# A ten-stage float32 transformer kernel: retention's value products and MLA's rotary scores moved from plain float32 to split fp32r products

## The reference, cut to what matters

```python
# MLA, 8 heads: 128 "nope" + 64 rotated features; the rotated key is shared by all heads
q = concatenate([q[..., :128], _rope(q[..., 128:], positions, 10000.0)])
k_pe = _rope(ckv[..., None, 256:], positions, 10000.0)
k = concatenate([k[..., :128], broadcast_to(k_pe, (b, s, 8, 64))])
s = einsum('bqhd,bkhd->bhqk', q_blk, k) * scale      # causal, softmax over k

# retention, 4 heads of key width 256 and value width 512
a = einsum('bhid,bhjd->bhij', qi, ki) * d_intra      # decayed scores
inner = einsum('bhij,bhjv->bhiv', a, vi)             # the values product
...
return (silu(g) * group_normed(y)) @ w_out
```

## Time and profile before

| | |
|---|---|
| time, median of 3 runs | 2537.4 us (2537.21 to 2538.32) |
| the profiled execution's span, first to last instruction | 2535.6 us |
| PE busy | 2519.6 us, 99% |
| POOL busy | 1057.3 us, 42% |
| DVE busy | 997.8 us, 39% |
| ACT busy | 854.4 us, 34% |
| HBM traffic | 230.8 MB, 91 GB/s |
| granted TensorE clock, mean | 0.999 |

### The profile page before, as it was taken

One profiled execution on the slowest core, in us unless ns is written; L12 is line 12 of the kernel. 1 busy time (PEld: TensorE's weight loads), 2 busy tenths in 40 slices (PEclk: granted clock), 3 DMA queues, 4 the chain that ended last, 5 costly groups with the idle time before them and its releaser, 6 DMA issues.

```text
span 2535.6 us, 32083 instructions
## 1 busy us (share of the span) xinstructions
PE 2519.6 (99%) x12155; PEld 2085.4 (82%) x12155; DVE 997.8 (39%) x1795; ACT 854.4 (34%) x1225; POOL 1057.3 (42%) x824
## 2 busy tenths in 40 slices
PE   9999999999999999999999999999999999999998
PEld 7778888888888888888888888888877877888887
DVE  5556444457576344345234222223123023322223
ACT  4444222234565222235234222223232222422222
POOL 4224444444333444444333444444443433444443
PEclk9999999999999999999999999999999999999999
DMA  5212233223213322332221322223322322232222
GB/s 173 69 54 85 99 100 99 93 73 117 74 62 98 100 88 94 99 100 84 83 67 51 125 91 99 99 99 108 100 76 75 100 67 83 92 100 99 97 88 81
DMA packets 164732, 230.78 MB, mean 91 GB/s; under 512 B 14102, under 2 KB 130844, under 8 KB 164508
## 3 DMA queue, kind: packets, MB, share of 16 engines
q1 hardware_dynamic: 164636, 229.43, 27.9%
HBM read 227.32 MB, written 2.10 MB: 90 GB/s over the span
## 4 chain that ended last, share of the span: by engine, by line
PE 50%; issue 30%; POOL 18%; DVE 1%; DMA 0%; POOLq 0%; ACT 0%; SPq 0%
POOL w_lo L669 18%; PE bank L695 8%; PE bank L697 8%; PE bank L696 8%; PE bank L706 4%; PE bank L708 4%; PE bank L707 4%; PE bank L1486 2%; PE bank L1485 2%; PE bank L1487 2%; PE bank L1511 1%; PE bank L1498 1%; PE bank L762 1%; PE bank L962 1%; PE bank L960 1%
## 5 line engine op out<-in xcount | busy, mean ns | idle before, releaser
L669 POOL TENSOR_TENSOR w_lo<-w_raw,w_hi 128x512 fp32r<-128x512 f32 (+1 forms) x820 | 1057.1, 1321 | 1456.0 <-ACT w_hi L1638 1456.0
L1638 ACT ACTIVATE w_hi<-w_raw 128x2048 fp32r<-128x2048 f32 (+1 forms) x205 | 392.3, 1914 | 636.9 <-PE bank L708 390.4
L695 PE MATMUL bank<-h_hi,w_hi 128*128 128x512 f32 x1472 | 575.8, 391 | 0.0
L697 PE MATMUL bank<-h_hi,w_lo 128*128 128x512 f32 x1472 | 572.9, 389 | 0.0
L696 PE MATMUL bank<-h_lo,w_hi 128*128 128x512 f32 x1472 | 572.8, 389 | 0.0
L2172 DVE TENSOR_TENSOR x_residual<-x_residual,bank 128x512 f32<-128x512 f32 x455 | 310.5, 686 | 360.8 <-PE bank L708 313.2
L706 PE MATMUL bank<-w_hi,act_hi 128*128 128x512 f32 x952 | 371.3, 390 | 0.0
L708 PE MATMUL bank<-w_hi,act_lo 128*128 128x512 f32 x952 | 370.4, 389 | 0.0
L707 PE MATMUL bank<-w_lo,act_hi 128*128 128x512 f32 x952 | 370.4, 389 | 0.0
L695 PEld LDWEIGHTS bank<-h_hi,w_hi 128*128 128x128 f32 x1472 | 276.4, 188 | 62.1 <-issue 4.9
L697 PEld LDWEIGHTS bank<-h_hi,w_lo 128*128 128x128 f32 x1472 | 276.3, 188 | 57.9
(11 more groups left out here) (266 smaller groups left out, 2965.4 us busy)
## 6 DMA issues: line engine op xcount, KB each, us to landing
w_raw<-in_ffn_w_in SPq DMA_DIRECT2D x44, 1024.0 KB, 5.1
w_raw<-in_ffn_w_up SPq DMA_DIRECT2D x32, 1024.0 KB, 5.3
w_raw<-in_ffn_w_down SPq DMA_DIRECT2D x32, 1024.0 KB, 4.8
w_raw<-in_ret_w_in SPq DMA_DIRECT2D x24, 1024.0 KB, 5.1
w_raw<-in_ffn_w_out SPq DMA_DIRECT2D x22, 1024.0 KB, 4.8
w_raw<-in_diff_w_qkv SPq DMA_DIRECT2D x12, 1024.0 KB, 5.2
w_raw<-in_fox_w_in SPq DMA_DIRECT2D x12, 1024.0 KB, 5.3
w_raw<-in_ret_w_out SPq DMA_DIRECT2D x8, 1024.0 KB, 5.0
```

The costliest lines, as they stand in the source:

```text
L669: nc.gpsimd.tensor_tensor(m.w_lo[:, sl, at], m.w_raw[:, sl, at], m.w_hi[:, sl, at].bitcast(F32), ALU.subtract)\
L695: mm(out, hi, x[0][:, k, :], start=k == 0, stop=False)
L697: last = mm(out, lo, x[0][:, k, :], start=False, stop=k == kc - 1)
L1638: m.nc.scalar.activation(m.w_hi[:, sl, 0:width], m.w_raw[:, sl, 0:width], ACT.Copy).then_inc(m.sem("w_hi_ready"), 1)
```

## The change

In MLA, `q_two[:, j]` (fp32r) replaces the shared `q_pe` as stationary operand: head j's 64 rows hold the high part of its rotated queries, and the other 64 rows hold their low part. `k_pe` is filled in both heads' rows, and split into `k_high` and `k_rest` once. Two fp32r products per tile, over `k_high` and `k_rest`, replace the plain float32 product. VectorE makes `q_two` at the end of `take_rotated`: two copies of 128x512 and four subtractions of 32x512 whose output partitions differ from their input partitions.

In retention, the decayed scores are split (ScalarE high, VectorE low, in pieces of 512, 512 and 256 columns) and the values are split (ScalarE's eviction writes the high part, VectorE subtracts to get the low part from the bank). Three fp32r products replace each plain one. The two big fp32r buffers are shared by both uses, `work` shrinks, several temporaries move to `tokbuf` (also those of diff and retention rotations), and small column tiles are put together. The positions' second load moves behind `ln0_done`.

```diff
@@ constants
+RA_PARTS = ((0, 512), (512, 512), (1024, 256))
+RA_READY = (1, 3, 4)
@@ memory
+    m.r_hi, m.r_lo = sb("split_hi", [P, 2048], F32R), sb("split_lo", [P, 2048], F32R)
-    work = sb("work", [P, 11520])
+    work = sb("work", [P, 8192])
...
-    m.q_pe, m.k_pe = view(3072, 512), (view(3584, 512), view(5376, 512))
+    m.q_pe, m.k_pe = view(3072, 512), view(3584, 512)
+    m.q_two = m.r_hi[:, 0:1024].rearrange("p (a b) -> p a b", a=2)
+    m.k_high, m.k_rest = m.r_hi[:, 1024:1536], m.r_hi[:, 1536:2048]
...
+    m.rv_hi, m.rv_lo = (r[:, :].rearrange("p (t d) -> p t d", t=TT) for r in (m.r_hi, m.r_lo))
+    m.ra_hi, m.ra_lo = (a[:, 4:7, :].rearrange("p a b -> p (a b)") for a in (m.act_hi, m.act_lo))
@@ SyncE, beside_ffn0
         sp.wait_ge(*m.upto("mla_rope_made", 2))
+        sp.wait_ge(*m.upto("ln0_done", TT))
         sp.dma_start(m.pos.bitcast(I32), d["positions"].broadcast_to([P, T])).then_inc(s("pos_in"), 16)
-        sp.wait_ge(*m.upto("ln0_done", TT))
         layernorm_rows("ffn", 0)
@@ pe_scores
-        pe.wait_ge(*m.upto("mla_pe_in", p + 1))
+        pe.wait_ge(*m.upto("mla_pe_low", 4 * p + 2 * j + 2))
         if head == 0:
-            pe.wait_ge(*m.upto("k_pe_in", 4))
+            pe.wait_ge(*m.upto("k_pe_rest", 1))
...
-            last = mm(out, m.q_pe[:, tile], m.k_pe[j][:, 0:w], start=False, stop=True)
+            mm(out, m.q_two[:, j, tile], m.k_high[:, 0:w], start=False, stop=False)
+            last = mm(out, m.q_two[:, j, tile], m.k_rest[:, 0:w], start=False, stop=True)
@@ pe_retention, tokens (x == "g") and values
-                    left("v_in", TT, t + 1)
+                    left("v_lo", TT, t + 1)
...
-            left_before("decayed", TT, TT)
-            left_before("v_in", TT, TT)
+            left_before("ra_lo", 3, 3)
+            left_before("v_lo", TT, TT)
...
-                    last = mm(b[2 + q][:, :], m.ra[:, at:at + P], m.rv[:, kb, :], start=kb == 0, stop=kb == q)
+                    hi, lo = m.ra_hi[:, at:at + P], m.ra_lo[:, at:at + P]
+                    mm(b[2 + q][:, :], hi, m.rv_hi[:, kb, :], start=kb == 0, stop=False)
+                    mm(b[2 + q][:, :], hi, m.rv_lo[:, kb, :], start=False, stop=False)
+                    last = mm(b[2 + q][:, :], lo, m.rv_hi[:, kb, :], start=False, stop=kb == q)
@@ act_retention
+        def decays_high():
+            for n, (at, w) in enumerate(RA_PARTS):
+                left_before("decayed", TT, RA_READY[n])
+                run(m.ra_hi[:, at:at + w], m.ra[:, at:at + w], ACT.Copy).then_inc(s("ret_ra_hi"), 1)
+
         if project:
             if hs[0]:
                 split([f"ret.k{n}" for n in hs])
+            if attend:
+                decays_high()
             split([f"ret.v0{n}" for n in hs])
+        else:
+            decays_high()
...
-                    run((m.rv if x == "v" else m.rg)[:, t, :], ...
+                    run((m.rv_hi if x == "v" else m.rg)[:, t, :], ...
@@ dve_start
-    for j in range(2):
-        v.memset(m.k_pe[j], 0.0).then_inc(s("pe_clear"), 1)
...
-            v.tensor_tensor(m.k_pe[j][dst, :], turned[src, :], crossed[src, :], ALU.add).then_inc(s("k_pe_in"), 1)
+            v.tensor_tensor(m.k_pe[dst, :], turned[src, :], crossed[src, :], ALU.add).then_inc(s("k_pe_in"), 1)
+    dve.wait_ge(*m.upto("k_pe_in", 4))
+    v.tensor_copy(m.k_high, m.k_pe).then_inc(s("k_pe_high"), 1)
+    dve.wait_ge(*m.upto("k_pe_high", 1))
+    v.tensor_tensor(m.k_rest, m.k_pe, m.k_high.bitcast(F32), ALU.subtract).then_inc(s("k_pe_rest"), 1)
@@ dve_pairs, end of take_rotated
         v.tensor_tensor(m.q_pe, turned, crossed, ALU.add).then_inc(s("mla_pe_in"), 1)
+        dve.wait_ge(*m.upto("mla_pe_in", p + 1))
+        for j in range(2):
+            v.tensor_copy(m.q_two[:, j, :], m.q_pe).then_inc(s("mla_pe_high"), 1)
+        for j in range(2):
+            dve.wait_ge(*m.upto("mla_pe_high", 2 * p + 2))
+            for half in range(2):
+                src = slice(64 * half + 32 * j, 64 * half + 32 * j + 32)
+                dst = slice(64 * half + 32 - 32 * j, 64 * half + 64 - 32 * j)
+                v.tensor_tensor(m.q_two[dst, j, :], m.q_pe[src, :], m.q_two[src, j, :].bitcast(F32), ALU.subtract).then_inc(s("mla_pe_low"), 1)
@@ dve_retention, after the decays, and after take("k") and the lows
+            for n, (at, w) in enumerate(RA_PARTS):
+                left_before("ra_hi", 3, n + 1)
+                v.tensor_tensor(m.ra_lo[:, at:at + w], m.ra[:, at:at + w], m.ra_hi[:, at:at + w].bitcast(F32), ALU.subtract)\
+                    .then_inc(s("ret_ra_lo"), 1)
...
+            for tile in range(TT):
+                dve.wait_ge(*m.upto("ret_v_in", along(i, [TT * h + tile + 1 for h in hs])))
+                v.tensor_tensor(m.rv_lo[:, tile, :], b[(0, 1, 6, 7)[tile]][:, :], m.rv_hi[:, tile, :].bitcast(F32), ALU.subtract)\
+                    .then_inc(s("ret_v_lo"), 1)
```

More of the change, by code:

```diff
@@ L403, in memory @@
     m.q, m.k, m.v = view(0, 1024, 2), view(1024, 1024, 2), view(2048, 1024, TT)
-    m.q_pe, m.k_pe = view(3072, 512), (view(3584, 512), view(5376, 512))
+    m.q_pe, m.k_pe = view(3072, 512), view(3584, 512)
+    m.q_two = m.r_hi[:, 0:1024].rearrange("p (a b) -> p a b", a=2)
+    m.k_high, m.k_rest = m.r_hi[:, 1024:1536], m.r_hi[:, 1536:2048]
     m.probs, m.probs2, m.turned = view(4096, 1280), view(5376, 1280), view(6656, 1280)
-    m.tmp = view(7936, 1536, 3)
+    m.tmp = view(3072, 1024, 2)
+    m.rot_tmp = [tok[:, 512 * n:512 * n + 512] for n in range(2)]
+    m.k_pe_tmp = [m.turned[:, 512 * n:512 * n + 512] for n in range(2)]
+    m.diff_tmp = [tok[:, 512 * n:512 * n + 512] for n in range(4)]
     m.sel = view(5376, 1024, 8)
     m.sel_r, m.c_rows = m.act_hi[:, 2:4, :].rearrange("p a (b n) -> p (a b) n", n=P), m.act_hi[:, 4, :]
-    m.rv, m.rg, m.ra, m.ry, m.rtmp = view(2048, 2048, TT), view(4096, 2048, TT), view(6144, 1280), view(7424, 2048, TT), view(9472, 2048, 4)
+    m.ry, m.rg, m.ra = view(2048, 2048, TT), view(4096, 2048, TT), view(6144, 1280)
+    m.rv_hi, m.rv_lo = (r[:, :].rearrange("p (t d) -> p t d", t=TT) for r in (m.r_hi, m.r_lo))
+    m.ra_hi, m.ra_lo = (a[:, 4:7, :].rearrange("p a b -> p (a b)") for a in (m.act_hi, m.act_lo))
     m.relu, m.square = view(0, 1024, 2), view(1024, 1024, 2)
@@ L412, in memory @@
     m.squares, m.centered = view(4096, D), view(4096 + D, 2 * D, 2)
-    m.rb_q = view(9472, 512)
-    m.pos, m.ang, m.turns = view(9984, 512), view(10496, 512), view(11008, 512)
+    m.rb_q = tok[:, 1536:2048]
+    m.pos, m.ang, m.turns = view(6656, 512), view(7168, 512), view(7680, 512)
     m.rb = sb("rstd_rows", [P, T])
     m.rope_cos, m.rope_sin = sb("rope_cos", [P, T]), sb("rope_sin", [P, T])
+    m.ret_tmp = [tok[:, 2 * D:2 * D + T], tok[:, 2 * D + T:3 * D], m.rope_cos[:, :], m.rope_sin[:, :]]
     m.consts = sb("consts", [P, 6 * P + 4])
@@ L425, in memory @@
     m.neg_max, m.row_sum, m.row_rec = sb("neg_max", [P, 8]), sb("row_sum", [P, 8]), sb("row_rec", [P, 8])
-    m.o_sq, m.o_eps, m.o_std, m.o_rstd = sb("o_sq", [P, TT]), sb("o_eps", [P, 2, TT]), sb("o_std", [P, TT]), sb("o_rstd", [P, TT])
+    o = sb("o_columns", [P, 5 * TT])
+    m.o_sq, m.o_std, m.o_rstd = (o[:, TT * n:TT * n + TT] for n in range(3))
+    m.o_eps = o[:, 3 * TT:5 * TT].rearrange("p (n t) -> p n t", n=2)
     m.lam_in, m.lam = sb("lam_in", [P, 4, 64]), sb("lam", [P, 8])
@@ L429, in memory @@
     m.wf, m.wf_hi, m.wf_lo = sb("wf", [P, KC, 8]), sb("wf_hi", [P, KC, 8], F32R), sb("wf_lo", [P, KC, 8], F32R)
-    m.x_sum, m.x_sq = sb("x_sum", [P, 2 * TT]), sb("x_sq", [P, TT])
-    m.x_neg_mean, m.x_std, m.x_rstd = sb("x_neg_mean", [P, TT]), sb("x_std", [P, TT]), sb("x_rstd", [P, TT])
+    xc = sb("x_columns", [P, 6 * TT])
+    m.x_sum, m.x_sq = xc[:, 0:2 * TT], xc[:, 2 * TT:3 * TT]
+    m.x_neg_mean, m.x_std, m.x_rstd = (xc[:, TT * n:TT * n + TT] for n in (3, 4, 5))
     m.b_f, m.gate_f, m.c_cols = sb("b_f", [P, 8]), sb("gate_f", [P, 6, TT, 8]), sb("c_cols", [P, TT, 8])
-    m.y_stats, m.y_mean = sb("y_stats", [P, TT, 6]), sb("y_mean", [P, TT, 2])
-    m.y_std, m.y_rstd, m.y_shift = sb("y_std", [P, TT]), sb("y_rstd", [P, TT]), sb("y_shift", [P, TT])
+    y = sb("y_columns", [P, 11 * TT])
+    m.y_stats, m.y_mean = (y[:, at:at + TT * n].rearrange("p (t n) -> p t n", t=TT) for at, n in ((0, 6), (6 * TT, 2)))
+    m.y_std, m.y_rstd, m.y_shift = (y[:, TT * n:TT * n + TT] for n in (8, 9, 10))
     return m
@@ L2018, in step @@
                     act.wait_ge(*m.upto("blocks_done", block_done(i, names, t)))
-                    run((m.rv if x == "v" else m.rg)[:, t, :], b[(0, 1, 6, 7)[t]][:, :], ACT.Copy if x == "v" else ACT.Silu)\
+                    run((m.rv_hi if x == "v" else m.rg)[:, t, :], b[(0, 1, 6, 7)[t]][:, :], ACT.Copy if x == "v" else ACT.Silu)\
                         .then_inc(s(f"ret_{x}_in"), 1)
@@ L2133, in dve_start @@
     dve.wait_ge(*m.upto("mla_rope_made", 2))
-    turned, crossed = (m.tmp[:, n, :] for n in range(2))
+    turned, crossed = m.k_pe_tmp
```

(7 more changed lines are left out.)

## The result

The kernel with the change takes **2542.6 us** (median of 20 runs, 2539.1 to 2545.0) against 2538.0 for the kernel before (20 runs beside them, 2537.0 to 2540.3): ratio **1.0016** with a 95% interval of 1.0010 to 1.0021. It is 4.6 us slower (2.5 to 5.3 by the interval). The forecast was 2534.6, range 2530 to 2539. The profiled execution of after has a span of 2540.8 against 2535.6, so the two traces show the whole difference: +5.2.

The account below looks back on a forecast made before the run. PE, busy 99% of the span, was taken as the bound. Products saved 7.2 us in MLA and 6.7 in retention, waits on VectorE added 11.1: -2.8 from 2537.4 gave 2534.6 us, 8-in-10 range 2530 to 2539.

Parts of the forecast that it names:

- the products: MLA and retention: fp32r products in place of plain float32 save 7.2 us over 8 heads and 6.7 us over four.
- the three waits: MLA: PE waits 3.7 us each for VectorE before head 0's scores and the values of heads 1 and 5.
- the one that is covered: MLA pair 2, before head 4's scores: VectorE's new work is hidden with 0.6 us to spare, cost 0.
- the clock's term: MLA: the forecast's sum held no time for TensorE's clock falling behind the new waits.
- rival 3: MLA: TensorE's clock falls in the new waits, about 3 us a fall, three giving 2543.6 us; chance 0.08.
- the load of the positions: SP's queue: later load delays one weight load by half a microsecond, its consumer behind a whole MLP group; costed at nothing.
- The other zeros: Other new work, in MLA and retention, costed at nothing; at most 0.5 us or at worst 1 for some.
- The key split at the start: Copy and subtraction at about 41 us, beside POOL: cover 0.4 us, at most 0.5 paid if it is gone.
- retention's splits: Retention: splits of the decayed scores fit behind the q projection or, in the last head, 24 products; cost 0, at worst 1.
- the values' low part: Retention: four subtractions per head from PSUM in a quiet VectorE, each needed 8 us later; costed at nothing.

Follow-up runs that it names:

- the kernel with the load moved alone: Changed kernel with the positions' load put behind the first MLP's first down weights on SP's queue; 2539.7 us, ratio 1.0007 to the kernel before.
- the kernel with both orders changed: Changed kernel with VectorE's split halved per head, PE's next first query product ahead of head 0's scores, positions' load behind the down weights; 2526.2 us, ratio 0.9954.

## Why the prediction was wrong

**Right: the products.** MLA 0.90 a head forecast, 0.89 measured; retention 1.7 a head forecast, 8.58 - 6.80 = 1.78 measured, 7.1 in all instead of 6.7. The term was short since the product's pitch was rounded up to 0.23; thirty of them took 6.80.

**Right: the three waits and the one that is covered.** 3.7 each forecast, 3.55 to 3.63 measured, at the places named; head 4 has none. VectorE's block took 3.66 (forecast 3.8).

**Wrong step 1: the clock's term was nothing, and rival 3 had a chance of 0.08.** This is the error that turned the sign: the sum -7.2 - 6.7 + 11.1 has no term for the clock behind its three waits. The mechanism and the price were in the text: one fall about 3 us, three falls +9. What was measured is three falls and 7.8 us. The argument against it was that the clock "held for about the first half" of the window after the kernel's last product. The clock record of before shows what that was worth: its last product ended at 2527.83 and the clock fell at 2533.11, 5.3 us later. In after the same end took 3.0 us (2532.95 to 2535.99), and the pauses 2.8 to 3.5. Over the eleven traces the delay behind the last product is 2.0 to 5.3 us, and before's is the longest of them. The delay is not one number, and a single reading at its long end was taken as a safe bound for waits of 3.7. The trace of before alone could not show the spread, but one reading was no reason for 0.08. The Trainium skill, page "TensorE: Matmul & The Clock Gate", section "Part 1: The HAM clock gate", says that the throttled state is the default and activity releases it; the nine falls in nine pauses agree, and the prediction had set that rule aside because no row showed it in so short a pause.

**Wrong step 2: the load of the positions at nothing.** "Its consumer is behind a whole MLP group" is true, and its cover was some 1.3 us, which was not read from the trace. The weights came 2.0 us later, not half a microsecond, and POOL's four instructions took 6.58 us where a group that meets no such VectorE work takes 5.04 to 5.06. In that stretch VectorE's two-SBUF-input instructions took 1.78 and 1.66 us instead of 0.69. This contention is no new cost: the same four took 6.11 in before, and 6.12 in the kernel with the load moved alone, where the wait is down to 0.2. The Trainium skill, page "SBUF — State Buffer", section "Who interferes with whom", describes that exclusion; these rows agree. Measured: 1.2 us, and the load's place is what decides it.

**The other zeros held.** The key split at the start, retention's splits and the values' low part brought no wait into PE's list.

With the measured terms the sum closes to 0.2 us: -7.1 - 7.1 + 10.8 + 7.8 + 1.2, less 0.55 ahead of MLA (25.89 against 26.44 for the same product, a lead that several other executions don't have), is +5.05; the spans differ by 5.2.

## What to carry to other kernels

A wait put into a TensorE stream that was full costs its length and then, from a few microseconds on, the clock: here 10.8 us of waiting brought 7.8 more. Waits of 3.4 us brought a fall each time and waits of 1.65 to 1.85 once in four, so price a fall behind each new wait of that length, and ask first whether the operation that feeds the next product can be cut in two, with only the needed half ahead of it: the same work in another order, with the load of the positions moved too, turned 1.0016 into 0.9954. And "its consumer is far behind" is a number to read, not a reason for a zero.

## What the runs showed of the hardware

- The granted clock fell to half in stretches of 3.41 or 6.83 us, 15 of them in the middle of the kernel over all profiles. The fall can come after the pause has ended (by 0.1 to 1.2 us, in five of the ten falls at pauses); it came 2.2 to 4.7 us after the last product before the pause. By half of PE's busy time in the stretch, an estimate, a fall behind a pause cost 1.6 to 3.2 us.
- The clock also fell with PE at work. In fox ten plain float32 products of only 8 columns (20 records) run back to back for about 2 us, and PE counts as busy; in five of the eleven profiles the clock fell within 1.3 us of their end, for 3.41 us, with no pause of PE in the 15 us before, and in six it did not. No edit touched this part of the kernel. Here PE's timeline of the kernel with both orders changed, whose fall is at 1186.04:

```profile
1183.74 0.81 PE L1374 MATMUL bank<-gate_f,ones 128*128 128x8 f32 x6
1184.41 0.37 PE L1374 MATMUL bank<-gate_f,consts 128*128 128x8 f32 x2
...
1186.43 0.41 PE L725 MATMUL bank<-w_lo,h_hi 128*128 128x256 f32 x1
```

  The 256-column product takes 0.41 there and 0.28 before the fall. That the narrow products are the cause was not tested. It is worth 1.7 us, and it is a likely part of the spread of every kernel here.
- The subtractions from SBUF to SBUF on 32 shifted partitions take 2.83 us for four with fp32r output, the same as the float32 additions; the rounding copies took 0.42 for one and 0.76 for two.
